# Meta tokens' 16x16 system by forward substitution, 16-row products padded to 128, ends of stages reordered

## The reference

```python
a_mat = jnp.where(strict, jnp.einsum('bhncd,bhnsd->bhncs', k_beta, k) * decay, 0.0)
sol = lax.linalg.triangular_solve(a_mat + eye, rhs, left_side=True, lower=True, unit_diagonal=True)
...
    v_new = w_val_c - jnp.einsum('bhck,bhkv->bhcv', w_key_c, S)
    o = jnp.einsum('bhck,bhkv->bhcv', q_dec_c, S) + jnp.einsum('bhcs,bhsv->bhcv', qk_c, v_new)
    S = S * g_last_c[..., None, None] + jnp.einsum('bhck,bhcv->bhkv', k_dec_c, v_new)
...
mix = jax.nn.sigmoid(gate_a) * (y_a @ w_o_gdn) + jax.nn.sigmoid(gate_b) * (y_b @ w_o_fox)
h = h + mix @ w_out
```

## Time and profile before

| | |
|---|---|
| median of 3 runs | 2924.84 us (2921.94 to 2925.22) |
| profiled execution | 2926.05 us, span 2924.4 us, mean granted clock 0.99 |
| PE / PEld busy | 2869.2 us (98%) / 2568.0 us |
| DVE busy | 1994.7 us (68%) |
| ACT busy | 1430.2 us (49%) |
| POOL busy | 276.9 us (9%) |
| chain that ended last | PE 94%, issue 2%, POOL 2%, DVE 1%, ACT 1%, DMA 1% |

### The profile page before, as it was taken

One profiled execution on the slowest core, in us unless ns is written; L12 is line 12 of the kernel. 1 busy time (PEld: TensorE's weight loads), 2 busy tenths in 40 slices (PEclk: granted clock), 3 DMA queues, 4 the chain that ended last, 5 costly groups with the idle time before them and its releaser, 6 DMA issues.

```text
span 2924.4 us, 52660 instructions
## 1 busy us (share of the span) xinstructions
PE 2869.2 (98%) x18731; PEld 2568.0 (88%) x18731; DVE 1994.7 (68%) x3460; ACT 1430.2 (49%) x2496; POOL 276.9 (9%) x229
## 2 busy tenths in 40 slices
PE   7999999999999899999999999999999999999998
PEld 7999999999999788888888888888888998888877
DVE  6767677676767565665776665656777667778865
ACT  5555565556555444443454443444544554445543
POOL 0000000000000000001550000000270002400014
PEclk9999999999999899999999999999999999999999
DMA  5434444343434255556555565565655454554445
GB/s 192 148 123 130 135 133 133 128 134 130 141 121 138 93 186 187 186 187 201 184 177 194 179 195 186 179 194 179 194 179 180 159 166 146 185 162 149 146 136 172
DMA packets 128957, 472.88 MB, mean 162 GB/s; under 512 B 14368, under 2 KB 14368, under 8 KB 128672
## 3 DMA queue, kind: packets, MB, share of 16 engines
q1 hardware_dynamic: 126144, 459.46, 48.2%
q0 software_dynamic: 2656, 11.33, 1.2%
HBM read 468.50 MB, written 2.24 MB: 161 GB/s over the span
## 4 chain that ended last, share of the span: by engine, by line
PE 94%; issue 2%; POOL 2%; DVE 1%; ACT 1%; DMA 1%; POOLq 0%; DVEq 0%; ACTq 0%
PE bank L287 35%; PE bank L288 18%; PE bank L289 10%; PE bank L290 9%; PE bank L291 9%; PE bank L729 1%; PE bank L801 1%; PE bank L780 1%; PE bank L797 1%; POOL late_sum L436 1%; POOL late_sq L432 1%; PE bank L958 1%; PE bank L1117 0%; PE bank L850 0%; PE bank L1035 0%
## 5 line engine op out<-in xcount | busy, mean ns | idle before, releaser
L263 DVE TENSOR_TENSOR w_lo<-raw,w_hi 128x1024 fp32r<-128x1024 f32 x866 | 1062.7, 1253 | 178.5 <-ACT w_hi L257 167.9
L257 ACT ACTIVATE w_hi<-raw 128x1024 fp32r<-128x1024 f32 x866 | 898.1, 1052 | 471.1 <-PE bank L288 457.1
L287 PE MATMUL bank<-u,w_hi 128*128 128x512 f32 x2288 | 818.4, 400 | 3.2 <-DVE ya L1842 3.2
L289 PE MATMUL bank<-u,w_hi 128*128 128x272 f32 (+2 forms) x2064 | 641.1, 311 | 8.4 <-DVE w_lo L263 6.7
L288 PE MATMUL bank<-u,w_lo 128*128 128x256 f32 x2288 | 645.3, 282 | 0.0
L287 PE MATMUL bank<-ya,w_hi 128*128 128x512 f32 x1792 | 636.1, 400 | 0.0
L290 PE MATMUL bank<-u,w_hi 128*128 128x272 f32 (+2 forms) x2064 | 590.4, 286 | 0.0
L291 PE MATMUL bank<-u,w_lo 128*128 128x272 f32 (+2 forms) x2064 | 590.1, 286 | 0.0
L287 PEld LDWEIGHTS bank<-u,w_hi 128*128 128x128 f32 x2288 | 431.5, 189 | 102.7 <-issue 6.8
L288 PE MATMUL bank<-ya,w_lo 128*128 128x256 f32 x1792 | 504.1, 281 | 0.0
L288 PEld LDWEIGHTS bank<-u,w_lo 128*128 128x128 f32 x2288 | 433.9, 190 | 0.4
(11 more groups left out here) (366 smaller groups left out, 3284.1 us busy)
## 6 DMA issues: line engine op xcount, KB each, us to landing
raw<-in_stream SPq DMA_DIRECT2D x868, 512.0 KB, 3.4
mix_row<-rows POOLq DMA_DIRECT2D x16, 408.0 KB, 3.9
xT<-in_xT SPq DMA_DIRECT2D x4, 544.0 KB, 6.2
h<-in_xT POOLq DMA_DIRECT2D x1, 2048.0 KB, 9.5
out_dram<-h SPq DMA_DIRECT2D x4, 512.0 KB, 2.6
consts<-in_consts POOLq DMA_DIRECT2D x1, 1921.0 KB, 9.4
vecs<-in_vecs POOLq DMA_DIRECT2D x1, 166.5 KB, 7.0
consts<-in_consts POOLq DMA_DIRECT2D x1, 137.0 KB, 5.9
```

What stands on the lines that cost most here:

```text
L257: act.activation(w_hi[:, slot], raw[:, slot], ACT.Copy).then_inc(hi_ready, 1)
L263: dve.tensor_tensor(w_lo[:, slot], raw[:, slot], w_hi[:, slot].bitcast(F32), ALU.subtract).then_inc(lo_ready, 1)
L287: pe.matmul(o, a, x, start=first, stop=False)
L289: pe.matmul(o, a, x[:, 0], start=first, stop=False)
```

## The change

1. The meta chunk leaves the doubling. The 16x16 spans of `pe_transpose`, `pe_prod` and `pe_step` go; all levels work on 128 columns. The transpose becomes PE's own transpose, one record instead of four.
2. Its system is solved on VectorE by forward substitution over 16 columns, in the transposed layout (128 value channels on the partitions): one scaling of `vT` and 15 steps, 8 of them and the scaling between level 4 and `f out`, 7 between mask 5 and level 5. Coefficients are `b_mat[0:16, 0:16]`, which POOL writes to DRAM and reads back broadcast to all partitions. `pe_meta_v` becomes a transpose of the result. The meta chunk's v is no longer transposed or scaled (one transpose on PE, one ACTIVATE less).
3. The other 16-row products (`pe_meta_state`, first product of `pe_fox_out`) read tiles of 128 rows whose lower 112 are zeroed once at the start (4 memsets on VectorE). The 16-column product of `pe_kk` now has 128 rows out; level 64's products have 128 rows out.
4. Merge's gate tiles stand two outputs ahead (`MERGE`). The first four (64 blocks) run in the tail of mix, with splits, sums and tanh woven into the plans' windows.
5. VectorE's wait for `late inputs in` moves behind the splits of the first tile of out.
6. `mla_out` and `swa_out` issue 14 of their first tile's 16 blocks in the windows behind the last heads; the last two wait for the last head's output.
7. `row free` moves from `dve_qk` to the substitution; POOL's loop is unrolled.

```diff
+            def meta_coefficients(n):
+                gp.wait_ge(sem("b mat"), 4 * n - 3)
+                gp.dma_start(meta_rows, b_mat[0:META, 0:META]).then_inc(sem("meta coef"), 16)
+                gp.wait_ge(sem("meta coef"), 32 * n - 16)
+                if n > 1:
+                    gp.wait_ge(sem("meta step"), META * (n - 1))
+                gp.dma_start(coef_m[:].rearrange("p j i -> p (j i)"), meta_rows.rearrange("j i -> (j i)")
+                             .partition_broadcast(P)).then_inc(sem("meta coef"), 16)
...
-                for t0, w in MAIN_FIRST:
-                    mm = pe.matmul(bank[5][0:w, t0:t0 + w], kT[:, t0:t0 + w], kT[:, t0:t0 + w], start=True,
-                                   stop=True)
-                mm.then_inc(sem("kk"), 1)
+                for t0, w in MAIN:
+                    pe.matmul(bank[5][0:w, t0:t0 + w], kT[:, t0:t0 + w], kT[:, t0:t0 + w], start=True, stop=True)
+                pe.matmul(bank[5][:, 0:META], kT[:, 0:P], kT[:, 0:META], start=True,
+                          stop=True).then_inc(sem("kk"), 1)
...
-                for t0, w in FOLDED:
-                    mm = pe.matmul(bank[5][0:w, t0:t0 + w], inv[0:w, 0, t0:t0 + w],
-                                   const("identity", t0, t0 + w, w), start=True, stop=True)
-                mm.then_inc(sem("prod sum"), 1)
+                pe.transpose(bank[5][:, main], inv[:, 0, main], ident).then_inc(sem("prod sum"), 1)
...
-                for t0, w in level_spans(lv):
-                    mm = pe.matmul(bank[5][0:w, t0:t0 + w], b_mat[0:w, t0:t0 + w], part[0:w, 1, t0:t0 + w],
-                                   start=True, stop=True)
-                mm.then_inc(sem("prod sum"), 1)
+                pe.matmul(bank[5][:, main], b_mat[:, main], part[:, 1, main], start=True,
+                          stop=True).then_inc(sem("prod sum"), 1)
...
-                pe.wait_ge(sem("inverse"), 16 * n - 8)
-                pe.wait_ge(sem("v beta"), 3 * n)
+                pe.wait_ge(sem("meta step"), META * n)
+                pe.wait_ge(sem("v beta"), 2 * n)
                 pe.wait_ge(sem("yb lo"), n)
-                pe.matmul(bank[3][:, 0:P], inv[0:META, 0, 0:P], v_beta_m[:, :], start=True,
-                          stop=True).then_inc(sem("v new m sum"), 1)
+                pe.transpose(bank[3][0:META, 0:P], solve_m[:, :], ident).then_inc(sem("v new m sum"), 1)
...
-                blocks_left = mix_products(head) if head < HEADS else iter(())
+                blocks_left = mix_products(head) if head < HEADS else early_gates()
...
-                stream_ = mla_products(w) if w < PAIRS else iter(())
+                stream_ = mla_products(w) if w < PAIRS else first_blocks("mla_out", ya, KT - 2, ("mla lo", PAIRS - 1))
...
-                stream_ = swa_products(w) if w < KT else iter(())
+                stream_ = swa_products(w) if w < KT else out_left
...
+            def dve_meta(n, part_):
+                if part_ == 0:
...
+                    dve.scalar_tensor_tensor(out=solve_m[:], in0=vT[:, 0:META], scalar=0.5, in1=row[:, 0, 0:META],
+                                             op0=ALU.mult, op1=ALU.mult).then_inc(sem("meta step"), 1)
...
+                    dve.sem_inc(sem("row free"), 1)
+                    dve.wait_ge(sem("meta coef"), 32 * n)
+                for j in (range(8), range(8, META - 1))[part_]:
+                    dve.wait_ge(sem("meta step"), META * (n - 1) + 1 + j)
+                    dve.scalar_tensor_tensor(out=solve_m[:, j + 1:], in0=coef_m[:, j, j + 1:],
+                                             scalar=solve_m[:, j:j + 1], in1=solve_m[:, j + 1:], op0=ALU.mult,
+                                             op1=ALU.subtract, reverse1=True).then_inc(sem("meta step"), 1)
...
                     ahead(phase, 2 * t + 2)
+                    if phase == "out" and not t:
+                        dve.wait_ge(sem("late inputs in"), 32)
...
-            dve.wait_ge(sem("late inputs in"), 32)
```

More of the change, by code:

```diff
@@ L80, with merge_order @@
 TABLE, SLABS = phase_table()
+GATES_AHEAD = 2
+def merge_order():
+    order = [(x, i) for i in range(GATES_AHEAD) for x in ("gate a", "gate b")]
+    for i in range(KT):
+        order += [("gdn", i), ("fox", i)]
+        if i + GATES_AHEAD < KT:
+            order += [("gate a", i + GATES_AHEAD), ("gate b", i + GATES_AHEAD)]
+    return order
+MERGE = merge_order()
+EARLY_GATES = 2 * GATES_AHEAD
+EARLY_BLOCKS = EARLY_GATES * KT
 STREAM = -(-(SLABS + 2) // RING) * RING
@@ L1359, in mix_stream, with gate_tanh, gate_stream @@
                         act.activation(dest[x], proj[b][:, 0:dest[x].shape[1]], ACT.Copy).then_inc(tile_free[b], 1)
+            def gate_tanh(t):
+                b, turn = tile_no("merge", t)
+                act.wait_ge(tile_free[b], turn + 2)
+                x = gate_tile(*MERGE[t])
+                act.activation(x, x, ACT.Tanh, scale=0.5).then_inc(sem("silu tanh"), 1)
+            def gate_stream(upto, done):
+                for k in range(done, upto):
+                    if k % HALF_KT == 0 and k < EARLY_BLOCKS:
+                        split_hi(act, "merge", k // HALF_KT + 2)
+                    if k % KT == 3 and k > 3:
+                        gate_tanh(k // KT - 1)
             for head in range(HEADS + 1):
@@ L1380, in mix_high @@
                 act.activation(mx_x[:, k, 0, :], mix_v[:, None, :], ACT.Copy, scale=0.5).then_inc(sem("mix hi"), 1)
-            for i in range(KT):
-                for j in range(MERGE_TILES):
-                    ahead("merge", 8 * i + 2 * j + 2)
-                    if i and not j:
-                        mix_high(i - 1)
-                    if j < 2:
-                        b, turn = tile_no("merge", 4 * i + j)
-                        act.wait_ge(tile_free[b], turn + 2)
-                        x = (sig_a, sig_b)[j]
-                        act.activation(x[:], x[:], ACT.Tanh, scale=0.5).then_inc(sem("silu tanh"), 1)
+            for t in range(EARLY_GATES, len(MERGE)):
+                x, i = MERGE[t]
+                ahead("merge", 2 * t + 2)
+                if x == "gdn" and i:
+                    mix_high(i - 1)
+                if x in ("gate a", "gate b"):
+                    gate_tanh(t)
             mix_high(KT - 1)
@@ L1651, in dve_conv @@
                         dve.wait_ge(sem("v turned"), n - 1)
+                        dve.wait_ge(sem("meta step"), META * (n - 2) + 1)
                     elif x == "q":
@@ L1883, in mix_stream, with sum_halves, gate_out, gate_stream @@
                         split_lo(dve, "mix", head * MB + k // HALF_KT + 2)
+            def sum_halves(o, b):
+                return dve.tensor_reduce(o, proj[b][:].rearrange("p (a n) -> p n a", a=2), AX.X, ALU.add)
+            def gate_out(t):
+                await_slab(dve, "merge", 2 * t + 1)
+                b, _ = tile_no("merge", t)
+                if t < EARLY_GATES:
+                    dve.wait_ge(sem("v turned"), HEADS)
+                    dve.wait_ge(sem("meta step"), META * (HEADS - 1) + 1)
+                sum_halves(gate_tile(*MERGE[t]), b).then_inc(tile_free[b], 1)
+            def gate_stream(upto, done):
+                for k in range(done, upto):
+                    if k % HALF_KT == 0 and k < EARLY_BLOCKS:
+                        split_lo(dve, "merge", k // HALF_KT + 2)
+                    if k % KT == 1 and k > 1:
+                        gate_out(k // KT - 1)
             for head in range(HEADS + 1):
```

277 lines of the change are left out of this document (161 added, 116 removed).

## The result

| | before | after |
|---|---|---|
| median of 5 runs | 2924.84 us | 2874.36 us (2873.87 to 2875.22) |
| ratio | | 0.9829, 95% interval 0.9816 to 0.9843 |
| profiled span | 2924.4 us | 2872.8 us |

What follows compares the result with a forecast made beforehand. PE was taken to set the pace in mix. Terms 31.8 + 18.8 - 0.6 + 11.5 + 6.8 + 1.6 = 69.9 us off 2926.05 gave 2856.1, predicted median 2855 us, ratio 0.976; 8-in-10 range 2834 to 2888.

Steps and rivals of the forecast that it cites:

- rival A: VectorE becomes the bound of a head, substitution operations taking 0.3 us: 2878 us; chance 0.20 with other VectorE losses.
- First half of a head: PE up to a head's last block: smaller or fewer products save 1.99 us a head, 31.8 us over 16.
- Second half: PE's part in the next head's window: 1.25 us saved a head, times 15, 18.8 us.
- I cost this at nothing: Substitution on VectorE at 0.2 us an operation: level 5 starts about 0.3 late, PE needs it three blocks later.
- The 0.2 of 1.6 us in levels 2 to 4: PE could save 1.6 us a head there, but waits for VectorE; only 0.2 taken, bounds 0.1 and 1.6.
- Rival B: VectorE yields in levels 2 to 4 if soft and split slip behind: 21 us more, 2834 us; chance 0.12.
- Tail of mix: End of mix, with merge's first 64 blocks run inside it: net gain 11.5 us.
- Out: Stage out: the second tile's 5.51 us wait and its half clock go; gain 6.8 us, bounds 4 and 8.
- SWA and MLA: Stage ends with early output blocks: SWA gains 1.6 us, MLA taken as 0, bounds -2 and 1.
- The coefficients' cover: POOL's queue: 41 places give 22 us, two broadcasts and issues take about 9; hidden, 13 us to spare.
- Rival C: Coefficients come late and stop PE for 15 heads, slower than before; at 28 us of transfers 2940 us; chance 0.04.
- Rival D: Padding does nothing, only removed 16x16 products count: loses 13.6 us, 2869 us; upper part inside the forecast's 0.62.

Runs made afterwards that it cites:

- experiment 3: Kernel after the change with meta state and FoX's first product reading 16 of the 128 rows again: 2878.6 us, ratio 0.9834.
- experiment 1: Kernel after the change with the 15 substitution steps left out, scaling and coefficient transfers kept: 2857.7 us, ratio 0.9760.
- experiment 2: Kernel after the change with the same substitution operations spread in groups over places where VectorE idles: 2854.2 us, ratio 0.9758.
- experiment 4: VectorE's level 3 put before the 1.2 us split, on the kernel after: 2875.6 us; with mask 4 too, on the spread-substitution kernel: 2843.8 us.
- Experiment 5: Kernel after the change with ScalarE's four gate tanh moved later and the Ln/Exp table preloaded behind the third: 2867.4 us, ratio 0.9795.
- experiment 9: Kernel after plus spread steps, moved tanh and preload, early `ya` tile, later memsets, earlier ScalarE split: 2844.2 us; level 3 and mask 4 before the split too: 2833.9 us.
- experiment 8: Two runs on the kernel after: memsets moved behind the scalars' sign, 2870.1 us; `mla_out` and `swa_out` without early blocks, 2869.6 us.
- experiment 7: Kernel after the change with POOL writing the coefficients to DRAM four extra times, each waited for, before the used write: 2869.9 us, ratio 0.9815.
- experiment 6: Kernel after the change with the first `ya` merge tile begun at 15 heads, only its last block awaiting the 16th: 2864.9 us, ratio 0.9797.

## Why the prediction was right, and which terms were mis-sized

The measured 2874.4 us lie in the range, but just outside the 2840 to 2872 us of the forecast itself, and nearer to rival A (2878) than to 2855. One of A's signs came: level 5 has no idle time in front of it, and PE is held up at product 6 (0.25 us to the next block instead of 0.14) and at meta v. Of the signs of being right, the operations 0.2 us apart did not come, and mix's last block ends 39.5 us earlier, where some 50 were named. So the mechanism on PE was right, the wait on VectorE was under-priced, and that the range holds is owed to A's price in it.

**First half of a head, 31.8 us forecast: right.** 2.01 us a head measured against 1.99. The price list by start-to-start times carries over to the new shapes, but for `pe_kk`: its 128-row product with 16 columns costs the expected 0.14 us (867.02 to 867.16), while the 16x16 one had cost 0.24 there and not 0.32. The drain rule of the Trainium skill (TensorEngine Tiling (Array Packing), Key Properties), by which `pe_kk` would save too, is not told apart here. `pe_kk` saved 0.10 us; experiment 3 agrees with the rule, since not only the 16-row product but also the ones ahead of it and, in FoX, behind it cost more.

**Second half, 18.8 us forecast, about 9 measured.** This is the largest miss. The savings on PE were even under-sized (1.25 against the 1.56 of experiment 1): each of the three 16-row products also cost 0.09 on the product ahead of it (experiment 3), which a price from its own start to the next does not see. Level 64 with its 64 rows out is the same case: it takes 0.37 us to the next block before and after (935.92 to 936.29, 898.48 to 898.85), but the product ahead of it took 0.22 us and takes 0.12, so it saved 0.10 instead of 0.15. The step that failed is "I cost this at nothing" for the substitution: it costs 0.95 us a head, 14 us in 15 heads. The mechanism and its threshold stand in the prediction: each 0.1 us on an operation costs 1.6 us a head from about 0.21 us. The sixteen operations took 4.23 us (2.55 + 1.68) where 16 x 0.21 are 3.36. The 0.87 us above that is close to the 0.95 that experiments 1 and 2 found. Two things were mis-sized. One is the operation's price, taken as 0.2 after the 0.19 from a reciprocal of two columns to its successor; it is 0.26 to 0.27, and the row of a 128x128 pair had 0.3. The other is the 0.53 us from the scaling to the first step, which no term had. The price lies nearer the upper bound, and rival A had the cause. Its "VectorE becomes the bound of a head" is too strong, though: experiment 2 keeps the work and loses nothing.

The 0.2 of 1.6 us in levels 2 to 4 was right in its reason: product 3 and product 4 wait 0.36 and 0.6 us in each head. Experiment 4 shows that half of what VectorE withheld (0.7 of 1.4 us a head) was its queue's order, a 1.2 us split in front of level 3 and mask 4. Rival B's condition, soft and split slipping behind, is met there by hand for the split: 0.7 us a head of the 1.4 it named.

**Tail of mix, 11.5 us forecast, about 5.4 measured.** The last block of mix ends at 935.9, PE starts on `ya` at 978.95: 43 us instead of 50.4, less 2 us for the half clock behind it. The sum step was forecast 32.5 us behind the last block and stands 37.9 behind it (973.83). Of these 5.4 us, 2.4 are PE's wait at meta state, 1.7 (estimate, from some 4 us at 1.2 GHz) the half clock behind that, 1 the substitution. What failed is that I looked for the gates' tanh only at the end of ScalarE's queue (0.8 us) and not at where the other three stand: the first is queued ahead of `v new m`, with a sum that VectorE gives late. Experiment 5 takes this stall away, and 7 us come, 2.7 of them in front of the sum step. The substitution had a part in it too: spread out (experiment 2), with the tanh where it was, it brings 3.1 us in front of the sum step, since PE's wait is 1.99 us instead of 2.41 and the clock stays at 1.00. Both together bring 3.9 us (experiment 9), so the two causes overlap. The last stretch, sum to `ya`, takes 5.1 us instead of 4.65: the load on this way is Exp's, not tanh's. The Trainium skill (ScalarE activation tables: per-element evaluation and per-set limits, Table sets in the compiler and the runtime) says that loads are placed by greedy longest run. The trace does not settle this rule. After a tanh, Ln and the Exp behind it got a load each, 1.28 us apiece, though one set holds both: with that set loaded ahead they needed none. Why the run was broken between them is open.

**Out, 6.8 us forecast: right.** Waits of 0.7 us in all, as forecast, no half clock, and 6.3 us gained. **SWA and MLA, 1.6 and 0:** 2.1 gained and 0.4 lost between these two traces, but by experiment 8 both are within the scatter of the clock. **Memsets, 0.6:** 0.6 us of operations, and 49.5 to 52.2 us at the next anchor, so this term can't be read from one trace. **The coefficients' cover: right.** In the head of experiment 7 the broadcast is issued at 874.3 and lands 13 us ahead of its first reader, 13 us to spare forecast. **Rival C** is refuted with up to 13.5 us added. The Trainium skill's port lock (SBUF — State Buffer, "SBUF: two separate sides") is not seen here either: the broadcast lands in 3.5 us with VectorE 78% busy. **Rival D** is refuted by experiment 3.

The sum, forecast against measured: 31.8 / 32, 18.8 / 9, tail 11.5 / 5.4, out 6.8 / 6.3, startup -0.6 / -2.1, SWA and MLA 1.6 / 1.7. The measured ones add up to 53; the spans differ by 51.6, and 1 us went in stages that the change does not touch.

## What to carry to other kernels

Work that is put into idle places of an engine is free only to the length of each place: price the dependent operation from a row of its own kind (self-dependent, same shape), compare group by group with each gap, and cut the work so that each group is shorter than its gap. Here that was worth 20 us without a single operation less. When a stage's last window gets new work, go through every engine's queue for what now stands in front of the critical steps, also where the added operation is short; its wait is what counts. A wait that moves on when one step is advanced (experiment 4) is no proof that the chain itself is the limit: move all that stands on the same side of the obstacle.

## What the runs showed of the hardware

- A self-dependent VectorE operation on 128x15 takes 0.27 us from start to start, nearly as long as the 0.31 us of a dependent 128x128 pair (883.77 to 884.08): the columns hardly count here.
- A 16-row product costs 0.28 us more than one of 128 rows up to its successor (0.42 against 0.14) and 0.09 on the product ahead of it; in FoX 0.19, 0.11 on its successor and 0.09 ahead. A product of 128 rows with 64 rows out cost 0.10 on the product ahead of it.
- 1 KB writes to DRAM on POOL's queue, each waited for, took 1.8 to 4.5 us to the next issue, with VectorE busy for 78% of the time.
- The same startup reached its first transposes between 49.5 and 52.2 us in different kernels. The mean granted clock from 18 us to there was 0.89 in the trace of experiment 6 (49.95 us) and 0.75 in that of the kernel after (52.02 us). The stage end behind MLA scattered by 2.7 us among kernels that have the same code there.
